# Nine modulation vectors of a two-layer decoder trunk: their partition sums taken by turning the totals and adding along the row

## The reference, cut to what matters

```
cs = jax.nn.silu(c)                                     # 1 x 1024
kv_mod = cs @ kv_ada_w + kv_ada_b                       # 2 vectors of 1024
mod = cs @ ada_w[layer] + ada_b[layer]                  # 6 vectors of 1024 for each layer
sh_m, sc_m, g_m, sh_f, sc_f, g_f = jnp.split(mod, N_MOD, axis=-1)
```

## Time and profile before

| | us |
|---|---|
| three timed runs | 2110.72, 2115.93, 2115.91 |
| median | 2115.91 |
| profiled execution, its own time | 2109.97 |
| span of its trace | 2108.2 |
| TensorE busy in the span | 2064.5 |
| VectorE busy in the span | 1602.1 |

### The profile page before, as it was taken

How to read it: one execution, slowest core, us unless ns; L and a number is a source line. 1 busy time by engine, 2 the same in 40 slices (tenths; PEclk the granted TensorE clock), 3 DMA queues, 4 the chain that set the end, 5 groups by cost and what they waited for, 6 DMA issues and landing times.

```text
span 2108.2 us, 28428 instructions
## 1 busy us (share of the span) xinstructions
PE 2064.5 (98%) x9676; PEld 1680.7 (80%) x9676; DVE 1602.1 (76%) x2422; ACT 941.5 (45%) x1594; POOL 246.9 (12%) x239
## 2 busy tenths in 40 slices
PE   6999999999999999999999999999999999999998
PEld 5888888888788888888887876677888888888886
DVE  7666565768887887887798956766888778778778
ACT  4211354245354355345467356545445534543552
POOL 0000221010000110110110022322001011011014
PEclk9999999999999999999999999999999999999999
DMA  7777653413454345336322510210454533533532
GB/s 303 260 258 221 124 106 131 134 46 127 176 197 152 130 156 188 112 138 209 140 81 72 193 58 11 81 60 31 140 218 141 199 119 119 209 129 119 190 139 80
DMA packets 111414, 300.40 MB, mean 142 GB/s; under 512 B 9360, under 2 KB 21824, under 8 KB 104160
## 3 DMA queue, kind: packets, MB, share of 16 engines
q1 hardware_dynamic: 103328, 276.86, 37.8%
q0 software_dynamic: 5232, 18.01, 4.0%
q10 hardware_dynamic: 2768, 4.41, 0.6%
HBM read 276.14 MB, written 23.10 MB: 142 GB/s over the span
## 4 chain that ended last, share of the span: by engine, by line
PE 90%; DVE 5%; ACT 2%; DMA 1%; issue 1%; POOL 1%; SPq 0%; ACTq 0%; DVEq 0%; POOLq 0%
PE ps L2597 27%; PE ps L2599 27%; PE ps L2598 27%; PE ps L3052 1%; PE ps L3084 1%; PE ps L3066 1%; PE ps L2617 1%; PE ps L2687 1%; DMA early_place<-in_early 1%; PE ps L2831 1%; PE ps L2816 1%; PE ps L2820 1%; DVE stats L1991 1%; DVE ulo L1948 1%; DVE wlo L1650 1%
## 5 line engine op out<-in xcount | busy, mean ns | idle before, releaser
L2597 PE MATMUL ps<-whi,uhi 128*128 128x512 f32 x704 | 288.8, 410 | 0.2 <-ACT resid L1488 0.2
L2599 PE MATMUL ps<-whi,ulo 128*128 128x512 f32 x704 | 276.2, 392 | 0.0
L2598 PE MATMUL ps<-wlo,uhi 128*128 128x512 f32 x704 | 275.6, 391 | 0.0
L2164 DVE TENSOR_TENSOR resid<-ps,resid 128x512 f32<-128x512 f32 x336 | 218.4, 681 | 22.6 <-PE ps L2599 21.4
L2597 PEld LDWEIGHTS ps<-whi,uhi 128*128 128x128 f32 x704 | 132.9, 189 | 36.3 <-issue 10.0
L2599 PEld LDWEIGHTS ps<-whi,ulo 128*128 128x128 f32 x704 | 132.8, 189 | 29.2
L2598 PEld LDWEIGHTS ps<-wlo,uhi 128*128 128x128 f32 x704 | 133.2, 189 | 24.9
L2599 PE MATMUL ps<-uhi,wlo 128*128 128x512 f32 x368 | 143.3, 389 | 0.0
L1053 ACT ACTIVATE whi<-stage 128x1024 fp32r<-128x1024 f32 x68 | 70.8, 1055 | 152.0 <-DMA stage<-in_stream 53.1
L968 POOL TENSOR_TENSOR wlo<-w_whole,whi 128x1024 fp32r<-128x1024 f32 x12 | 28.9, 2408 | 922.6 <-DVE hhi L2145 922.6
L1650 DVE TENSOR_TENSOR wlo<-stage,whi 128x1024 fp32r<-128x1024 f32 x68 | 82.9, 1232 | 45.7 <-ACT whi L1053 45.3
(11 more groups left out here) (402 smaller groups left out, 5320.0 us busy)
## 6 DMA issues: line engine op xcount, KB each, us to landing
stage<-in_stream SPq DMA_DIRECT2D x152, 512.0 KB, 4.5
hlo<-ulo_dram SPq DMA_DIRECT2D x56, 1024.0 KB, 4.8
ulo<-ulo_dram SPq DMA_DIRECT2D x40, 1024.0 KB, 5.3
scratch<-in_stream SPq DMA_DIRECT2D x33, 512.0 KB, 4.2
w_whole<-in_stream SPq DMA_DIRECT2D x28, 512.0 KB, 5.1
lnrows<-in_stream SPq DMA_DIRECT2D x25, 512.0 KB, 4.4
qk<-in_stream SPq DMA_DIRECT2D x24, 512.0 KB, 5.3
ulo_dram<-ulo SPq DMA_DIRECT2D x8, 1024.0 KB, 6.8
```

Source lines behind the costliest of these rows:

```text
L2164: v.tensor_tensor(dst, ps[:, down_bank(first, product, t), :], dst, ALU.add).then_inc(dve_evac, 1)
L2597: pe.matmul(dst, left_hi, right_hi, start=start, stop=False, skip_group_check=more)
L2598: pe.matmul(dst, left_hi, right_lo, start=False, stop=False, skip_group_check=more)
L2599: return pe.matmul(dst, left_lo, right_hi, start=False, stop=stop, skip_group_check=more)
```

## The change

`sum_vector` treats nine of the eleven vectors (`TURNED`, from SH_F0 to SH_F1 in the order of `SUMMED`) in another way: it turns each of the eight blocks of the total with TensorE's transpose, into the 1024 columns of banks 6 and 7. `take_mod` then adds 128 neighbouring columns each along the row with one `tensor_reduce` on VectorE, from 128 x 1024 in PSUM to `colsum` of 128 x 8, waits for it, and adds the bias as before. SC_M0 and SC_F1 stay with the ones.

Since each turned vector fills both banks, the next `sum_vector` waits until the last vector has been taken (`sum_read >= SUM_NUMBER[vec]`). G_F1 moves ahead: its last block of the total goes from tile 14 to tile 13 of the v stage, its sum stands after tile 14, its take after the evacuation of tile 15, and TensorE waits for that take ahead of the first output stage. `turn_p(0)` in the query stage waits for the take of SH_F1.

```
-SUM_BANK = {v: 6 + n % 2 for n, v in enumerate(SUMMED[1:8])} | {SH_F1: 7, SC_F1: 7}
+SUM_BANK = {SC_F1: 7}
+TURNED = SUMMED[1:10]
-            [(G_F1, 1, 2)], [(G_F1, 2, 4)], [(G_F1, 4, 5)], [(G_F1, 5, 7)], [(G_F1, 7, 8)], []]
+            [(G_F1, 1, 2)], [(G_F1, 2, 4)], [(G_F1, 4, 5)], [(G_F1, 5, 8)], [], []]
...
+        colsum = sb("colsum", [P, K])
...
             def take_mod(vec):
                 v.wait_ge(sum_done, SUM_NUMBER[vec] + 1)
-                dst = mods[:, vec, :]
-                v.tensor_tensor(dst, ps[:, SUM_BANK.get(vec, M), 0:K], dst, ALU.add).then_inc(sum_read, 1)
+                dst, src = mods[:, vec, :], ps[:, SUM_BANK.get(vec, M), 0:K]
+                if vec in TURNED:
+                    src = colsum[:]
+                    step.mark(v.tensor_reduce(src, ps[:, X + 2:X + 4, :].rearrange("p a (b n) -> p (a b) n", n=P),
+                                              axis=AXIS.X, op=ALU.add))
+                v.tensor_tensor(dst, src, dst, ALU.add).then_inc(sum_read, 1)
...
-                for vec in {0: (SH_KV,), 2: (SC_KV,), 4: (SH_M1,), 8: (SC_M1,), 10: (G_M1,)}.get(tile, ()):
+                for vec in {0: (SH_KV,), 2: (SC_KV,), 4: (SH_M1,), 8: (SC_M1,), 10: (G_M1,), 15: (G_F1,)}.get(tile, ()):
...
                 take_raw(c, 0)
-                if c == 0:
-                    take_mod(G_F1)
                 update(c, 0)
...
                 if vec != SC_M0:
-                    pe.wait_ge(sum_read, SUM_NUMBER[vec] - (1 if vec in SUM_BANK and vec != SC_F1 else 0))
+                    pe.wait_ge(sum_read, SUM_NUMBER[vec])
                 for k in range(K):
-                    last = pe.matmul(ps[:, bank, k:k + 1], total[:, k * P:(k + 1) * P], ones[:, 0:1], start=True,
-                                     stop=True)
+                    block = total[:, k * P:(k + 1) * P]
+                    if vec in TURNED:
+                        last = pe.transpose(ps[:, X + 2 + k // 4, k % 4 * P:(k % 4 + 1) * P], block, ident[:])
+                    else:
+                        last = pe.matmul(ps[:, bank, k:k + 1], block, ones[:, 0:1], start=True, stop=True)
                 last.then_inc(sum_done, 1)
...
-                    for vec in {1: (SC_KV,), 3: (SH_M1,), 7: (SC_M1,), 9: (G_M1,)}.get(T * nh + t, ()):
+                    for vec in {1: (SC_KV,), 3: (SH_M1,), 7: (SC_M1,), 9: (G_M1,), 14: (G_F1,)}.get(T * nh + t, ()):
                         sum_vector(vec)
...
-            pe.wait_ge(sum_read, SUM_NUMBER[G_M1] + 1)
+            pe.wait_ge(sum_read, SUM_NUMBER[G_F1] + 1)
...
                 numerators(c, 0)
-                if c == 0:
-                    sum_vector(G_F1)
                 by_token(FIRST["o0"] + c, W_O, c, part=(0, 1))
-                if c == 0:
-                    pe.wait_ge(sum_read, SUM_NUMBER[G_F1] + 1)
...
                 if n == 0:
                     pe.wait_ge(second_row_taken, 2)
+                    pe.wait_ge(sum_read, SUM_NUMBER[SH_F1] + 1)
```

More of the change, by code:

```diff
@@ L25 @@
 ACT = mybir.ActivationFunctionType
+AXIS = mybir.AxisListType
 P = 128
```

## The result

The changed kernel took 2143.06 us (median of four runs, 2142.18 to 2144.03), the kernel before 2115.91. The ratio is 1.0135, 95% interval 1.0122 to 1.0147: 28 us slower, where 7.9 were forecast, and outside the range of 2114 to 2130.

The account below looks back on a forecast made before the run. It took TensorE as the bound (busy 2064.5 of 2108.2 us). Waits and work of +4.5 us and clock drops of +3.4 made +7.9 us, giving 2123.8 us scaled to the median of 2115.91; range 2114 to 2130.

Parts of the forecast that it names:

- TensorE's own work, -0.3 us: Nine sums: eight turned blocks take 1.67 us instead of 1.70 for products with ones; bounds -1.1 and +0.5.
- faster: Rival: nothing takes off more than 1.1 us, so only the 5 us spread between runs could show it; chance 0.07.
- The reduction, 1.20 us, start to release 1.45: VectorE's new tensor_reduce takes 1.20 us; from start of a take to start of what waits for it, 1.45 us.
- SC_F0, +2.4: TensorE waits 2.4 us before the sum of SC_F0 for the take of SH_F0; bounds 1.9 to 3.7.
- SH_KV, +0.5: TensorE waits 0.5 us before the sum of SH_KV for the take of SC_F0; bounds 0 and 2.2.
- SH_M1, +0.1, bounds 0 and 2.0: The sum of SH_M1 waits 0.1 us for its total's last block, as two longer takes stand before that block.
- the loads carry the lateness: Rival: later takes delay loads, waits for loads recover nothing, SH_M1's block is 1.8 us late; +11.4 us, chance 0.08.
- The take at the boundary, +1.4: G_F1's take now stands behind the copy of tile 15, so TensorE goes on 1.4 us later; 1.0 to 2.7.
- SH_F1, +0.3: SH_F1's take before two VectorE passes of 1.6 us each makes TensorE wait 0.3 us more; 0 to 1.6.
- The clock, two drops, +3.4: Idle times of 2.4 us at 108 and 2.2 at 230 each drop the clock, losing 1.7 us each.

Follow-up runs that it names:

- e1: The changed kernel with its 32-byte tile colsum allocated last, no instruction changed: 2116.57 us, ratio 1.0008 to the kernel before.
- e2: The kernel before with an unused tile of 32 bytes where the change has colsum: 2138.71 us, ratio 1.0113.
- e3: The kernel before with an unused tile of 64 bytes where the change has colsum: 2139.96 us, ratio 1.0121.
- e4: e1 with SH_F0 and SC_F0 summed by products with ones again, SC_F0's sum not waiting for SH_F0's take: 2115.31 us, ratio 1.0005.
- e11: The kernel before with 32 unused bytes ahead of the first tile, so all tiles move together: 2115.30 us, ratio 0.9998.
- e9: The kernel before with small tiles moved last or merged, so gate_row and all behind it lie 256 bytes lower: 2116.49 us, ratio 1.0005.
- e10: The kernel before with 128 unused bytes ahead of the first tile, so all tiles move together: 2117.21 us, ratio 1.0003.
- e12: The kernel before with 32 unused bytes between hhi and hlo, so only h_whole and hlo are off a multiple of 256: 2123.35 us, ratio 1.0031.
- e6: The kernel before with 32 unused bytes ahead of ident and 96 behind gate_row, moving everything behind them by 128: 2135.21 us, ratio 1.0105.
- e7: The kernel before with only SC_KV, SC_M1 and G_M1 turned, colsum last, G_F1 where it was: 2116.21 us, ratio 1.0007.
- e5: The kernel before with an unused tile of 128 bytes where the change has colsum: 2135.37 us, ratio 1.0104.

## Why the prediction was wrong

The direction was right and the size was not, for a reason outside all of its steps. The two parts, measured: edits +1.7 us (e1), place of the tiles +24 to +25 (e2, e3), together about 26 to 27, and the interval of the whole is 25.8 to 31.1. The direction was luck. It came from the tiles, which the prediction doesn't have; the edits that it forecast at +7.9 can't be told from nothing, and its own sum with the turned blocks counted rightly (the second point below) is 4.8 - 8.2 + 3.4 = 0.0 us.

- **The step that failed is a term that was put at nothing without a reason: the pace of all products outside the sums.** The prediction's sum has terms for the sums, for the waits and for the clock. The one line of the diff that moves no instruction, `colsum = sb("colsum", [P, K])`, has none, and it moves every tile behind it by 32 bytes. The sum took for granted that a product of 512 columns costs what it cost before, wherever its operands lie. The runs showed in its place: steps of 228 to 239 ns instead of 226.7 wherever `hhi`, `hlo` or `ninth` takes part or is near; 26.5 us back when `colsum` goes behind the other tiles (e1); and 24 to 25 us lost when an unused tile of 32 or 64 bytes is put into the kernel before (e2, e3).
- **TensorE's own work, -0.3 us:** -8.2 was right. The step read one row of eight records as four blocks turned, since a product of 32-bit floats shows as two records. A turned block shows as one: the row is eight blocks, and 0.79 us is the whole sum, 9 x (0.79 - 1.70) = -8.2. The same count in the row, x8 for eight blocks, stands in the changed kernel. With this the bound of the rival *faster*, that nothing takes off more than 1.1 us, falls too.
- **The reduction, 1.20 us, start to release 1.45:** right. 1.187 to 1.216 us over nine; from 109.80 to 111.33 are 1.53 us.
- **SC_F0, +2.4:** 4.42 (3.68 in e1). That the sum waits for a late take is as told, but not what makes the take late. TensorE's last gate record ends at 108.07 before and at 106.91 after; the copy stands behind an addition to a total that had waited for its load:

```profile
107.44 1.28 DVE L1622 SCALAR_TENSOR_TENSOR acc<-qk,cs,acc 128x1024 f32<-128x1024 f32 x1 [1.03 <-DMA qk<-in_stream]
```

In the changed kernel that addition starts at 108.32, again behind a wait for its load (1.19 us). So the take moved from 108.92 to 109.80 with the loads, while TensorE arrived 1.1 us earlier, most of it because the sum of SH_F0 ahead of it is shorter: 2.4 + 0.9 + 1.1 = 4.4.
- **SH_KV, +0.5:** none in the profiled run (the small addition ends at 136.38, TensorE comes at 136.83), 0.92 in e1. Within its bounds of 0 and 2.2.
- **SH_M1, +0.1, bounds 0 and 2.0:** 1.09 us of turning start at 162.99 behind an idle time of 2.26; 1.45 in e1 and 1.63 in e4. Mis-sized. The last block ends at 161.65 + 1.28, 6.1 us later than before, and VectorE still waited 0.27 us for its load: VectorE did not catch up in its waits for loads. That fits the rival *the loads carry the lateness*, with its 1.8 us, though e3 and e11 wait 0.30 and 1.01 us there without any turning.
- **The take at the boundary, +1.4:** 2.16 - 0.78 = 1.38. Right. The last block of G_F1 adds 0.71 (0.54 in e1) that the step had at nothing.
- **SH_F1, +0.3:** 0.68 to 0.71 idle at that place against 0.20, so +0.5.
- **The clock, two drops, +3.4:** one drop, of 6.8 us around the stall of 4.42. TensorE works through 6.0 us of it, from 111.33 to 117.32, and loses 2.8: the eight blocks take 1.59 us and not 0.79, the ten products behind them 4.40 and not the 2.39 of the kernel before. There is none at 237 behind 2.16 us idle in this run, and one of 3.4 us there in e1. That the sum comes near is luck, by one drop too many and one too short. And the drop at about 30 us of the kernel before is missing in the changed one: they come and go from run to run. In the earlier trace rows the window of 1475 to 1478 holds only 0.04 us of idle time (3.00 - 2.96), not 0.94; the rest of that lay ahead of it.

Put together for e1, from its rows: -8.2 + 3.7 + 0.9 + 1.5 + 1.4 + 0.5 + 2.7 = +2.5 us, within the interval of the medians (-0.6 to 4.0). This does not close the account. The rows are of one execution of 2117.75 us, which is 7.8 above the one of the kernel before that they are compared with. Of the other 5.3 us, 0.5 is the wait for the last block of G_F1, and 3.2 are two more stretches of 3.4 us at the 1.2 GHz level, in the first 60 us and at 237; the kernel before in turn has two more such stretches behind 1200 us than e1. The rest isn't placed. What makes the difference between some us and 28 is the place of the tiles: e1 and the changed kernel run the same instructions 26.5 us apart.

## What to carry to other kernels

Read the allocations of a diff like its instructions: a new small tile ahead of large ones moves them all, and can cost more than the code that uses it. Give the tiles that TensorE reads in its long products the same start residue by 256 bytes (shown here for 512 columns in 32-bit floats only), and put small tiles last. When two traces differ in a stage that nobody edited, compare the step from one product to the next, pair by pair of operands, before looking for a wait: here the busy time went *up* with fewer records, and no list of waits would have shown it.

## What the runs showed of the hardware

- With all operands at one residue by 256 bytes a product of 512 columns starts every 226.7 ns (e9, e10, e11 and the kernel before); with `hhi`, `hlo` or `ninth` at another, the steps with them or beside them are 228 to 239 (e2, e12). Offsets of 32, 64 and 128 bytes between them cost nearly the same (1.13%, 1.21% and 1.04% of this kernel), and the residue itself is of no account (0, 32 and 128 for these tiles all gave the same time). The Trainium skill ("SBUF — State Buffer", section "Operand start alignment") asks only that an operand start at a multiple of its element size; all of these do, so they are allowed. It speaks of legality and not of speed, and here they are not equally fast.
- A block turned on TensorE in 32-bit floats costs 0.10 us in a row of eight (0.79 / 8), under half of the 0.21 of a product with ones (1.70 / 8).
- A reduction of 128 x 1024 from PSUM to 128 x 8 takes 1.19 to 1.22 us, as the pass with two operands does:

```profile
L1637 DVE TENSOR_REDUCE colsum<-ps x9: 1187/1212/1216, 109.8 to 1226.7; 128x8 f32<-128x1024 f32 x9
```

- A clock drop of 3.4 us followed the narrow sum of SC_F0 with no idle time in e4, e6 and e10, and that of SH_M1 with 0.41 us idle in e7 and none in e2 and e10; at the same places in the kernel before and in e5 there was none.
